# A hybrid decoder layer on one core: the MLP's up-projection as seven block products per pair of output tiles, in eighths

## The chip, the cores and the metric

One NeuronCore of one Trainium2 chip runs the whole kernel in one launch. The metric is the device time of an execution in microseconds. A profiled execution gives, besides, a trace of every instruction on the core's engines: PE (TensorE; PEld is its weight load), DVE (VectorE), ACT (ScalarE), POOL (GpSimd) and SP (SyncE, which here only issues DMAs).

## The reference

One layer of a decoder, float32 throughout: RMSNorm, a combined input projection, block-sparse attention and an mLSTM side by side, an output projection, a squared-ReLU MLP, and a final norm. The change concerns the last part. It works on 512 prompt tokens and 8 sample tokens, 520 in all; D_MODEL is 1024 and D_FF is 4096:

```python
    x = x + mix @ w_out
    hn = rmsnorm(x, ln2_w)
    x = x + jnp.square(jax.nn.relu(hn @ w_up)) @ w_down
```

## The kernel before

**Three passes.** Every float32 operand of a large matmul is split in two parts that TensorE reads in its fp32r format: `hi`, written by ACT as a copy into that format, and `lo`, the rest, written by DVE (or POOL) as a subtraction. A product is then three matmuls of 128x128 weights into one PSUM bank (`three`, L682 to L688): hi with hi, the activation's lo with the weight's hi, and the activation's hi with the weight's lo. Activations lie transposed, 128 features by 520 tokens, so a matmul streams tokens: 256 of them (half 0) or 264 (half 1).

**Output projection.** Eight output tiles of 128 features (groups G_OUT + j, j = 0 to 7), each in two token halves of 24 matmuls. A half is a slot; the program has 72 slots, and the last ones, 64 to 71, are tiles j = 4 to 7. Slots take three PSUM banks in turn, so a slot waits until the slot three before it has been added into `xT` by DVE (`evac_out`, L2070; counted by `s_acc_evac`). Behind an evacuated tile comes the task `x2` of that j: ACT writes `act_hi` (L1443) and a square `x_sq` (L1449), DVE writes `act_lo` (L2041) and adds the square into `sq_sum` (L2049).

**MLP.** Four quarters of 1024 hidden features. A quarter is 8 up tiles and 8 down tiles, each 8 k-steps times 2 halves times 3 passes, 48 matmuls (`main`, L716). The first up tile waits until all 72 slots are evacuated (`bank_free`), and is done k by k as `act_lo` comes. After it TensorE sums the squares over features (`sums_of_squares`, L1075), DVE scales the sums (L2111), POOL takes the power -1/2 (L1512), and TensorE spreads the result over partitions in the middle of the second tile (`norm_to_rows`, L1086); DVE copies it to `rstd2` (L2114). An up tile's PSUM is read by DVE with a ReLU and the factor `rstd2` into `relu` (L2132), squared twice by ACT (`relu2` L1484 and `h_hi` L1485), and `h_lo` is made by POOL (L1617). A down tile's PSUM is added into `xT` by DVE (L2076).

**Weights.** SP loads 1 MB at a time, 1024 rows by 256 columns, into one of two `raw` buffers. Each gives two weight tiles of 128x1024 elements, split by ACT (`weight_hi`, L1174) and DVE (`weight_lo`, L1181) three tiles ahead of TensorE into four slots. In the output projection POOL makes the lo parts, also those of the first three MLP tiles.

Every engine runs its own instructions in the order in which the program writes them, and waits on semaphores. Quarters 0 to 2 are a hardware loop on most engines, so counts that are waited for there are worked out in registers.

Of the kernel before, what the change touches and what calls it, by code (L numbers as in the profile page):

```python
# [264 lines left out]


# [1944 lines left out]
```

## Time and profile before

| | us |
|---|---|
| median of 3 runs | 758.96 |
| lowest, highest | 757.63, 759.50 |
| the profiled execution, its own time | 759.6 |
| its span, first to last instruction | 757.5 |
| granted TensorE clock, mean over the span | 0.987 |

| engine | busy us | share of the span |
|---|---|---|
| PE | 719.7 | 95% |
| DVE | 363.6 | 48% |
| ACT | 252.3 | 33% |
| POOL | 217.3 | 29% |

The profiled execution lies 0.6 us above the median of the runs, and 2.1 us of it lie outside its span. A matmul's duration (some 280 ns) is longer than the distance from its start to the next one's start, since matmuls follow each other in a pipeline; the distance is what counts for time. DVE and ACT instructions overlap their successors a little too.

### The profile page before, as it was taken

How to read it: one execution, taken by the hardware profiler on the slowest of the kernel's cores; microseconds unless marked ns; L12 is line 12 of the kernel's file. 1: busy time of each engine (PE TensorE's matmuls, PEld its weight loads, DVE VectorE, ACT ScalarE, POOL GpSimd, SP SyncE). 2: the span in 40 equal slices, each digit the busy share in tenths (PEclk: the TensorE clock that was granted, in tenths of full speed). 3: DMA queues.
4: the chain of work that ended last, by engine and by line, in shares of the span. 5: the costliest groups of instructions: out<-in, count | busy, mean ns of one | idle time of the engine just before them, and what ended most of it. 6: DMA issues, size and time to landing. Idle time of an engine off the chain costs nothing.

```text
span 757.5 us, 14708 instructions
## 1 busy us (share of the span) xinstructions
PE 719.7 (95%) x5729; PEld 670.3 (88%) x5729; DVE 363.6 (48%) x657; ACT 252.3 (33%) x424; POOL 217.3 (29%) x154
## 2 busy tenths in 40 slices
PE   5999789797999999899999999999999999999997
PEld 5988678676868676589999999999999999999996
DVE  4387878775353446435434333334333433333343
ACT  5342544535353213215324311342124322233312
POOL 6226987812232244163222100221002200022001
PEclk9999999998999999999999999999999999999999
DMA  7616898634456959623123332322331332313102
GB/s 241 209 56 211 270 279 250 191 125 117 146 155 202 282 193 163 221 86 106 62 60 110 112 112 62 106 92 77 111 109 58 111 94 72 112 57 111 57 1 112
DMA packets 94772, 100.37 MB, mean 133 GB/s; under 512 B 5374, under 2 KB 76626, under 8 KB 94714
## 3 DMA queue, kind: packets, MB, share of 16 engines
q1 hardware_dynamic: 80710, 92.91, 39.5%
q10 hardware_dynamic: 14004, 6.67, 3.7%
q8 instruction: 39, 0.64, 0.3%
q14 instruction: 19, 0.16, 0.1%
HBM read 92.92 MB, written 6.64 MB: 131 GB/s over the span
## 4 chain that ended last, share of the span: by engine, by line
PE 82%; DVE 7%; DMA 3%; ACT 2%; issue 2%; POOL 2%; SPq 1%; ACTq 0%; DVEq 0%; POOLq 0%
PE acc L684 23%; PE acc L685 22%; PE acc L686 22%; PE acc L1000 2%; DVE w_lo L1181 2%; DMA kv<-in_cache_v_dram 1%; PE scr L1050 1%; PE scr L931 1%; PE scr L944 1%; PE scr L1025 1%; ACT w_hi L1174 1%; DMA kv<-in_cache_k_dram 1%; PE scr L1038 1%; POOL sm_t L1512 1%; PE scr L775 1%
## 5 line engine op out<-in xcount | busy, mean ns | idle before, releaser
L684 PE MATMUL acc<-act_hi,w_hi 128*128 128x256 f32 (+1 forms) x928 | 269.1, 290 | 1.7 <-DVE zT L2056 1.1
L685 PE MATMUL acc<-act_lo,w_hi 128*128 128x256 f32 (+1 forms) x928 | 263.9, 284 | 0.0
L686 PE MATMUL acc<-act_hi,w_lo 128*128 128x256 f32 (+1 forms) x928 | 263.5, 284 | 0.0
L684 PEld LDWEIGHTS acc<-act_hi,w_hi 128*128 128x128 f32 x928 | 176.9, 191 | 9.1 <-issue 5.8
L685 PEld LDWEIGHTS acc<-act_lo,w_hi 128*128 128x128 f32 x928 | 176.9, 191 | 0.0
L686 PEld LDWEIGHTS acc<-act_hi,w_lo 128*128 128x128 f32 x928 | 176.4, 190 | 0.0
L1181 DVE TENSOR_TENSOR w_lo<-raw,w_hi 128x1024 fp32r<-128x1024 f32 x77 | 111.8, 1452 | 102.9 <-ACT w_hi L1174 102.5
L1174 ACT ACTIVATE w_hi<-raw 128x1024 fp32r<-128x1024 f32 x100 | 105.0, 1052 | 150.7 <-PE acc L686 147.2
L684 PE MATMUL acc<-h_hi,w_hi 128*128 128x264 f32 (+1 forms) x512 | 145.1, 283 | 0.0
L685 PE MATMUL acc<-h_lo,w_hi 128*128 128x264 f32 (+1 forms) x512 | 144.7, 283 | 0.0
L686 PE MATMUL acc<-h_hi,w_lo 128*128 128x264 f32 (+1 forms) x512 | 144.6, 282 | 0.0
L1617 POOL TENSOR_TENSOR h_lo<-relu,h_hi 128x520 fp32r<-128x520 f32 x32 | 42.1, 1316 | 277.3 <-ACT h_hi L1485 277.3
L684 PEld LDWEIGHTS acc<-h_hi,w_hi 128*128 128x128 f32 x512 | 96.6, 189 | 0.0
L685 PEld LDWEIGHTS acc<-h_lo,w_hi 128*128 128x128 f32 x512 | 96.5, 188 | 0.0
L686 PEld LDWEIGHTS acc<-h_hi,w_lo 128*128 128x128 f32 x512 | 96.3, 188 | 0.0
L1560 POOL TENSOR_TENSOR prod<-kv,Qb 128x1024 f32<-128x1024 f32 x32 | 82.9, 2617 | 42.6 <-DVE S L1759 25.2
L1181 POOL TENSOR_TENSOR w_lo<-raw,w_hi 128x1024 fp32r<-128x1024 f32 x23 | 54.9, 2390 | 105.6 <-ACT w_hi L1174 105.6
L2076 DVE TENSOR_TENSOR xT<-acc,xT 128x256 f32<-128x256 f32 x64 | 27.2, 428 | 84.7 <-PE acc L686 84.7
L1484 ACT ACTIVATE relu<-relu 128x520 f32<-128x520 f32 x32 | 20.4, 639 | 125.0 <-DVE relu L2132 125.0
L2056 DVE TENSOR_TENSOR zT<-acc,rstd 128x264 f32<-128x264 f32 (+1 forms) x56 | 23.5, 422 | 55.8 <-PE acc L686 52.7
L2132 DVE SCALAR_TENSOR_TENSOR relu<-acc,rstd 128x256 f32<-128x256 f32 x64 | 26.7, 421 | 40.1 <-PE acc L686 40.1
L684 PE MATMUL acc<-mix,w_hi 128*128 128x264 f32 (+1 forms) x128 | 37.7, 294 | 4.6 <-DVE mix L2022 3.2
(304 smaller groups left out, 823.1 us busy)
## 6 DMA issues: line engine op xcount, KB each, us to landing
kv<-in_cache_k_dram SPq DMA_DIRECT2D x64, 256.0 KB, 3.2
kv<-in_cache_v_dram SPq DMA_DIRECT2D x64, 256.0 KB, 3.5
raw<-in_w_up_dram SPq DMA_DIRECT2D x16, 1024.0 KB, 5.4
raw<-in_w_down_dram SPq DMA_DIRECT2D x16, 1024.0 KB, 5.1
raw<-in_w_in_dram SPq DMA_DIRECT2D x14, 512.0 KB, 6.0
raw<-in_w_in_dram SPq DMA_DIRECT2D x7, 1024.0 KB, 6.2
x_tok<-in_x_prompt_dram SPq DMA_DIRECT2D x8, 512.0 KB, 8.0
raw<-in_w_out_dram SPq DMA_DIRECT2D x4, 1024.0 KB, 7.5
```

The source lines that it names most:

```text
L684: pe.matmul(out, w_hi[:, slot, k, :], hi[k][:, cols], start=(n == 0), stop=False)
L685: pe.matmul(out, w_hi[:, slot, k, :], lo[k][:, cols], start=False, stop=False)
L686: mm = pe.matmul(out, w_lo[:, slot, k, :], hi[k][:, cols], start=False, stop=(n == KT - 1))
L1000: pe.matmul(acc[c:c + 32, 3, :], S_wide[:, b % 4, j, :], kv[:, j, :], start=(b % 4 == 0 and r == 0), stop=(b % 4 == 3 and r == 1)).then_in ...
L1174: act.activation(w_hi[:, slot, :, :], raw[:, r_slot, :, side * P:(side + 1) * P], ACT.Copy)\
L1181: eng.tensor_tensor(w_lo[:, slot, :, :], raw[:, r_slot, :, side * P:(side + 1) * P], w_hi[:, slot, :, :].bitcast(F32), ALU.subtract).then_ ...
L1484: act.activation(relu2[:, t % 2, :], relu[:, t % 2, :], ACT.Square)
L1560: pool.tensor_tensor(prod[:, n % 2, :].rearrange("p (j n) -> p j n", j=2), kv[:, 2 * c:2 * c + 2, :], Qb[:, b % 2:b % 2 + 1, :].to_broadca ...
L1617: pool.tensor_tensor(h_lo[:, t, :], relu2[:, t % 2, :], h_hi[:, t, :].bitcast(F32), ALU.subtract).then_inc(s_hs_lo, 1)
L2056: dve.tensor_tensor(zT[:, g, cols], acc[:, i % 3, 0:width(half)], rstd1[:, cols], ALU.mult)\
L2076: dve.tensor_tensor(x, acc[:, 2 * side + half, 0:width(half)], x, ALU.add).then_inc(s_acc_evac, 1)
L2132: dve.scalar_tensor_tensor(out=relu[:, t % 2, cols], in0=acc[:, 2 * (t % 2) + half, 0:width(half)], scalar=0.0, in1=rstd2[:, cols], op0=AL ...
```

## The change

Tokens are split in two halves of 260, the 1024 input features in two halves of four k-steps, and output tiles are taken in pairs. A pair is then a 2x2 by 2x2 block product. Before it took 8 block products of 12 matmuls (96 matmuls); now it takes 7 (84 matmuls), with sums of blocks on both sides (Strassen's scheme in the form with fewest sums):

- Weights: four sums of 128x512 blocks per pair (`w_sum`, DVE). A unit is now a 128x512 block or sum; ACT and DVE split each unit (`unit_hi`, `unit_lo`) into a ring of 11, and each unit serves one product of a pair or a half k-range of a down tile.
- Activations: in the task `x2` ACT also writes a scaled copy `xsc`, and for j = 4 to 7 DVE forms three sums of 128x260 (`t_tmp`), each of which ACT and DVE split too (`t2`, `t3`, `t4`); for j = 0 to 3 there is one difference (`t1_tmp`).
- Results: each product has a PSUM bank of its own (eight banks in turn). ACT copies the first to `p_copy`, and DVE makes seven additions of 128x260 per pair into `tmp0` and `tmp1`; the ReLU then reads these from SBUF, 520 wide.
- The MLP runs in eighths of 512 hidden features: up 0, up 1, down 0, up 2, down 1, and so on to down 5, up 7, and a last down phase over eighths 6 and 7 together. Down phases 0 to 5 accumulate over four k-steps only, so there are twice as many additions into `xT` for their features.
- The first 11 units are split in slots 65 to 71 of the output projection (`EARLY`), all of them by DVE. POOL has no weight split of the MLP any more.
- `sums_of_squares` now stands behind the third product, `norm_to_rows` behind the fifth.

```diff
-            def quarter(i, last):
...
+PAIR = ("A11", "A12", "S2", "S3", "S1", "S4", "A22")
+ORDER = [(what, side) for side in range(2) for what in PAIR]
+SUMS = {0: 1, 1: 2, 2: 3, 3: 4}
...
+PHASES = [("up", 0), ("up", 1)]
+for _d in range(6):
+    PHASES += [("down", _d)] + ([("up", _d + 2)] if _d < 6 else [])
+PHASES += [("last", 6)]
+RING = 11
...
+EARLY = {0: 65, 1: 65, 2: 66, 3: 66, 4: 67, 5: 68, 6: 68, 7: 70, 8: 70, 9: 71, 10: 71}
...
@@ PE
+            def up(e, i=0):
+
+                for m, (what, side) in enumerate(ORDER):
+                    n = FIRST["up", e] + m
+                    out = mlp_bank(BANKS["up", e, m][0])[:, 0:MH_TOK]
+                    bank_free("up", e, m, i)
+                    pe.wait_ge(s_u_lo, n + 1 + PER_LOOP * i)
+                    hi, lo = OPERAND[what]
+                    for k in range(4):
...
+                        pe.matmul(out, u_hi[n % RING][:, k, :], hi[k], start=(k == 0), stop=False)
+                        pe.matmul(out, u_hi[n % RING][:, k, :], lo[k], start=False, stop=False)
+                        mm = pe.matmul(out, u_lo[n % RING][:, k, :], hi[k], start=False,
+                                       stop=(k == 3))
+                    mm.then_inc(s_u_done, 1)
+                    if e == 0 and m == 2:
+                        sums_of_squares()
+                    if e == 0 and m == 4:
+                        norm_to_rows()
...
@@ DVE, task x2 from j = 4 on
+                        dve.tensor_tensor(t_tmp[:, 0, :], xsc[j][:, H1], xsc[k][:, H1], ALU.subtract).then_inc(s_t, 1)
+                        dve.wait_ge(s_t, made + 1)
+                        dve.tensor_tensor(t_tmp[:, 1, :], t_tmp[:, 0, :], xsc[k][:, H0], ALU.add).then_inc(s_t, 1)
+                        dve.wait_ge(s_x2_hi, j + 1)
+                        dve.tensor_tensor(act_lo[:, j, :], xsc[j][:, :], act_hi[:, j, :].bitcast(F32), ALU.subtract)\
+                           .then_inc(s_x2_lo, 1)
+                        dve.wait_ge(s_t, made + 2)
+                        dve.tensor_tensor(t_tmp[:, 2, :], xsc[j][:, H0], t_tmp[:, 1, :], ALU.subtract).then_inc(s_t, 1)
...
@@ DVE, a unit
+            def unit_lo(n, i=0):
+
+                kind, e, m, r = UNITS[n]
+                dve.wait_ge(s_u_hi, n + 1 + PER_LOOP * i)
+                dve.tensor_tensor(u_lo[n % RING], unit_source(n), u_hi[n % RING].bitcast(F32), ALU.subtract)\
+                   .then_inc(s_u_lo, 1)
+                if kind == "up" and m % 7 in SUMS:
+                    w_sum_of(e, SUMS[m % 7], m // 7, i)
...
@@ DVE, up
+                    if n == 2:
+                        dve.wait_ge(s_sums_up, 1)
+                        dve.tensor_scalar(rs[:, 0:NT], scr[:, 2, 0:NT], 1.0 / D, EPS, ALU.mult, ALU.add)\
+                           .then_inc(s_rs2_ms, 1)
...
```

The order that results, at three places on DVE. First the end of the output projection before, from the last-but-two additions into `xT` (slots 69 to 71, tiles 6 and 7) to the norm's scaling and copy:

```order
L2070 TENSOR_TENSOR xT<-acc,xT 128x264 [waits scr_free2,scr_free0,half_done]
L2070 TENSOR_TENSOR xT<-acc,xT 128x256 [waits scr_free2,scr_free1,half_done]
L2041 SCALAR_TENSOR_TENSOR act_lo<-xT,par,act_hi 128x520 [waits x2_hi]
L2049 TENSOR_TENSOR sq_sum<-sq_sum,x_sq 128x520 [waits sq_added,x1_sq]
L2070 TENSOR_TENSOR xT<-acc,xT 128x264 [waits scr_free2,scr_free1,half_done]
L2041 SCALAR_TENSOR_TENSOR act_lo<-xT,par,act_hi 128x520 [waits x2_hi]
L2049 TENSOR_TENSOR sq_sum<-sq_sum,x_sq 128x520 [waits sq_added,x1_sq]
L2111 TENSOR_SCALAR rs<-scr 128x4 [waits scr_full]
L2112 TENSOR_SCALAR rs<-scr 8x1
L2114 COPY rstd_62<-scr 128x512 [waits scr_full]
```

Between the additions of slots 70 (256 wide) and 71 (264 wide) stand one `act_lo` and one square.

The same place now, from the splits of the early units 7 and 8 through the addition of slot 71 (L2381) into the task x2 of tile 7 (buffer numbers are kept; `w_lo` and `u_lo` are places of the ring):

```order
L2413 TENSOR_TENSOR w_lo_52<-raw_49,w_hi_51 128x512 [waits u_hi]
L2398 TENSOR_TENSOR w_sum0_183<-raw_49 128x512 [waits u_lo]
L2413 TENSOR_TENSOR w_lo_52<-raw_49,w_hi_51 128x512 [waits u_hi]
L2401 TENSOR_TENSOR w_sum1_184<-w_sum0_183,raw_49 128x512 [waits w_sum,u_lo]
L2381 TENSOR_TENSOR xT_95<-acc,xT_95 128x264 [waits scr_free2,scr_free1,half_done]
L2341 TENSOR_TENSOR t_tmp_119<-xsc7_64,xsc3_60 128x260 [waits xsc]
L2343 TENSOR_TENSOR t_tmp_119<-t_tmp_119,xsc3_60 128x260 [waits t]
L2345 TENSOR_TENSOR act_lo_54<-xsc7_64,act_hi_53 128x520 [waits x2_hi]
L2348 TENSOR_TENSOR t_tmp_119<-xsc7_64,t_tmp_119 128x260 [waits t]
L2353 TENSOR_TENSOR t2_lo_139<-t_tmp_119,t2_hi_138 128x260 [waits t_hi]
L2353 TENSOR_TENSOR t3_lo_141<-t_tmp_119,t3_hi_140 128x260 [waits t_hi]
L2353 TENSOR_TENSOR t4_lo_66<-t_tmp_119,t4_hi_142 128x260 [waits t,t_hi]
```

Two splits and two weight sums stand ahead of slot 71's addition, and the task of tile 7 behind it is eight instructions instead of two.

Second, what follows on DVE up to the scaling of the sums of squares (L2510, L2512), where before `rs` stood right behind the last `sq_sum`:

```order
L2360 TENSOR_TENSOR sq_sum_82<-sq_sum_82,x_sq_81 128x520 [waits sq_added,x1_sq]
L2413 TENSOR_TENSOR w_lo_52<-w_sum1_184,w_hi_51 128x512 [waits u_hi]
L2403 TENSOR_TENSOR w_sum2_185<-raw_49 128x512 [waits u_lo]
L2413 TENSOR_TENSOR w_lo_52<-w_sum2_185,w_hi_51 128x512 [waits u_hi]
L2406 TENSOR_TENSOR w_sum3_186<-raw_49,w_sum1_184 128x512 [waits w_sum,u_lo]
L2413 TENSOR_TENSOR u_lo0_116<-w_sum0_183,u_hi0_113 128x512 [waits u_hi]
L2473 TENSOR_TENSOR tmp0_68<-acc,p_copy_69 128x260 [waits p_copy,u_done]
L2413 TENSOR_TENSOR u_lo1_117<-w_sum3_186,u_hi1_114 128x512 [waits u_hi]
L2473 TENSOR_TENSOR p_sum_70<-acc,p_copy_69 128x260 [waits u_done]
L2413 TENSOR_TENSOR u_lo2_118<-raw_49,u_hi2_115 128x512 [waits u_hi]
L2510 TENSOR_SCALAR rs_163<-scr 128x4 [waits sums_up]
```

Five unit splits, two weight sums and two additions of products moved in front of `rs`, whose first row is the last shown.

Third, the steady loop on DVE. Before:

```order
L1181 TENSOR_TENSOR w_lo<-raw,w_hi 128x1024 [waits w_hi_ok]
L2128 ISA
L2132 SCALAR_TENSOR_TENSOR relu<-acc,rstd_62 128x256 [waits half_done]
L2128 REGISTER_ALU
L2132 SCALAR_TENSOR_TENSOR relu<-acc,rstd_62 128x264 [waits half_done]
L1179 REGISTER_ALU
L1181 TENSOR_TENSOR w_lo<-raw,w_hi 128x1024 [waits w_hi_ok]
L2128 ISA
```

And now, in the middle of an up phase in the loop:

```order
L2412 REGISTER_ALU
L2413 TENSOR_TENSOR w_lo<-raw_d,w_hi 128x512 [waits u_hi]
L2482 REGISTER_ALU
L2473 TENSOR_TENSOR p_sum<-acc,p_copy 128x260 [waits u_done]
L2412 REGISTER_ALU
L2413 TENSOR_TENSOR w_lo<-raw_d,w_hi 128x512 [waits u_hi]
L2489 REGISTER_ALU [waits u_done]
L2473 TENSOR_TENSOR p_sum<-acc,p_sum 128x260 [waits c_ok]
L2492 REGISTER_ALU [waits u_done]
L2473 TENSOR_TENSOR tmp_67<-acc,p_sum 128x260 [waits c_ok]
L2473 TENSOR_TENSOR p_sum_71<-acc,p_sum 128x260
L2412 REGISTER_ALU
```

Each wait in the loop takes register instructions in both; now there are more and shorter instructions between them.

## Rows read from the trace of the kernel before

**Rows 1.** Windows: start:end, length; busy us (instructions) of PE, PEld, DVE, ACT, POOL; PEclk; DMA

```profile
353.50:373.50 20.00, 20.00 (x168) 19.87 (x166) 10.31 (x16) 9.55 (x14) 9.27 (x4) 1.00 0.33 107
374.00:750.00 376.00, 375.69 (x3133) 375.24 (x3133) 145.17 (x210) 105.09 (x138) 44.34 (x35) 1.00 0.26 82
```

**Rows 2.** Timeline of PE, both ends of a half tile: start us, duration us, instruction

```profile
500.38 0.28 PE L686 MATMUL acc<-act_hi,w_lo 128*128 128x256 f32 x1
500.50 0.28 PE L684 MATMUL acc<-act_hi,w_hi 128*128 128x264 f32 x1
...
503.29 0.28 PE L686 MATMUL acc<-act_hi,w_lo 128*128 128x264 f32 x1
503.41 0.28 PE L684 MATMUL acc<-act_hi,w_hi 128*128 128x256 f32 x1
```

**Rows 3.** DVE by line and shape, 400 to 725 us: xcount | busy us, mean ns | idle before

```profile
L1181 DVE TENSOR_TENSOR w_lo<-raw,w_hi 128x1024 fp32r<-128x1024 f32 x58 | 79.1, 1363 | 89.4 <-ACT w_hi L1174 89.4
L2132 DVE SCALAR_TENSOR_TENSOR relu<-acc,rstd 128x264 f32<-128x264 f32 x29 | 12.5, 432 | 38.6 <-PE acc L686 38.6
L2076 DVE TENSOR_TENSOR xT<-acc,xT 128x264 f32<-128x264 f32 x28 | 12.1, 433 | 57.8 <-PE acc L686 57.8
```

**Rows 4.** DVE by line and shape, whole span, inputs both in SBUF

```profile
L2017 DVE TENSOR_TENSOR zT<-zT 128x512 f32<-128x512 f32 x4 | 2.7, 684 | 0.0
...
L1899 DVE TENSOR_TENSOR S<-S,gate 128x256 f32<-128x256 f32 x2 | 0.9, 426 | 0.1
```

**Rows 5.** ACT and POOL by line and shape, 400 to 725 us

```profile
L1174 ACT ACTIVATE w_hi<-raw 128x1024 fp32r<-128x1024 f32 x57 | 59.9, 1051 | 107.5 <-PE acc L686 107.5
...
L1485 ACT ACTIVATE h_hi<-relu 128x520 fp32r<-128x520 f32 x29 | 18.0, 622 | 0.0
...
L1617 POOL TENSOR_TENSOR h_lo<-relu,h_hi 128x520 fp32r<-128x520 f32 x29 | 38.2, 1316 | 264.9 <-ACT h_hi L1485 264.9
```

**Rows 6.** Timeline of POOL and DVE: splits beside a POOL instruction and alone

```profile
499.63 1.32 POOL L1617 TENSOR_TENSOR h_lo<-relu,h_hi 128x520 fp32r<-128x520 f32 x1 [4.45 <-ACT h_hi L1485]
...
500.54 1.49 DVE L1181 TENSOR_TENSOR w_lo<-raw,w_hi 128x1024 fp32r<-128x1024 f32 x1 [2.26 <-ACT w_hi L1174]
...
429.85 1.23 DVE L1181 TENSOR_TENSOR w_lo<-raw,w_hi 128x1024 fp32r<-128x1024 f32 x1 [0.66 <-ACT w_hi L1174]
```

**Rows 7.** Timeline of DVE and PE, end of the output projection

```profile
357.15 0.68 DVE L2049 TENSOR_TENSOR sq_sum<-sq_sum,x_sq 128x520 f32<-128x520 f32 x1
357.76 0.42 DVE L2070 TENSOR_TENSOR xT<-acc,xT 128x264 f32<-128x264 f32 x1
...
370.70 0.42 DVE L2070 TENSOR_TENSOR xT<-acc,xT 128x256 f32<-128x256 f32 x1 [2.41 <-PE acc L686]
371.04 0.97 DVE L2041 SCALAR_TENSOR_TENSOR act_lo<-xT,par,act_hi 128x520 fp32r<-128x520 f32 x1
...
373.62 0.43 DVE L2070 TENSOR_TENSOR xT<-acc,xT 128x264 f32<-128x264 f32 x1 [1.00 <-PE acc L686]
...
374.15 0.36 PE L684 MATMUL acc<-act_hi,w_hi 128*128 128x256 f32 x1 [0.57 <-issue]
```

**Rows 8.** Norm of the MLP's input: chain (PE rows), then timeline of DVE and POOL

```profile
380.15 0.91 PE scr L1075 x10
...
384.10 1.20 PE scr L1086 x10
...
381.10 0.16 DVE L2111 TENSOR_SCALAR rs<-scr 128x4 f32<-128x4 f32 x1 [4.88 <-PE scr L1075]
...
385.02 0.69 DVE L2114 COPY rstd<-scr 128x512 f32<-128x512 f32 x1 [3.71 <-PE scr L1086]
...
381.46 1.52 POOL L1512 TENSOR_TENSOR rs<-rs,power 128x4 f32<-128x4 f32 x2 [9.99 <-DVE rs L2112]
```

**Rows 9.** Windows around an idle stretch of PE, columns as in the first group

```profile
168.00:175.00 7.00, 3.11 (x19) 1.77 (x17) 6.58 (x17) 0.00 (x0) 1.68 (x1) 1.00 0.00 0
175.00:183.00 8.00, 7.54 (x32) 6.87 (x33) 3.00 (x11) 4.14 (x11) 1.27 (x5) 0.57 0.61 164
```

More of the change, by code:

```diff
@@ new lines, with banks @@
+PREPARE = preparations()
+def banks():
+    use, last = {}, {b: ("out", N_HALVES) for b in range(3)}
+    last.update({b: ("scr", b - 4) for b in range(4, 8)})
+    for kind, e in PHASES:
+        if kind == "up":
+            for m, (what, side) in enumerate(ORDER):
+                b = m % 8
+                use[kind, e, m] = b, last.get(b)
+                last[b] = (("copy", 2 * e + side + 1) if what == "A11" else ("sum", 14 * e + 7 * side + READS[what]))
+                if e == 0 and m == 4:
+                    last[6] = last[7] = "rows", 2
+        else:
+            for j in range(16):
+                b = j % 4 if kind == "last" else (6 + j) % 8
+                use[kind, e, j] = b, last.get(b)
+                last[b] = "down", 16 * e + j + 1
+    return use
@@ L267 @@
+BANKS = banks()
+BANK_RATE = {"copy": 4, "sum": 28, "down": 32}
+for (_kind, _e, _n), (_b, _last) in BANKS.items():
+    if _kind != "last" and (_kind, _e) in PHASES[3:7]:
+        _b2, _last2 = BANKS[_kind, _e + 2, _n]
+        assert _b == _b2 and _last[0] == _last2[0] and _last2[1] - _last[1] == BANK_RATE[_last[0]]
+EARLY = {0: 65, 1: 65, 2: 66, 3: 66, 4: 67, 5: 68, 6: 68, 7: 70, 8: 70, 9: 71, 10: 71}
+N_DOWN = 16 * 6 + 16
 TASKS, JOBS = plan()
@@ new lines, in down_part @@
+            def down_part(b, half, n, k, first, last, signal):
+                out, cols = mlp_bank(b)[:, 0:MH_TOK], (H0, H1)[half]
+                w = u_hi[n % RING][:, k % 4, :], u_lo[n % RING][:, k % 4, :]
+                pe.matmul(out, w[0], h_hi[:, k, cols], start=first, stop=False)
+                pe.matmul(out, w[0], h_lo[:, k, cols], start=False, stop=False)
+                mm = pe.matmul(out, w[1], h_hi[:, k, cols], start=False, stop=last)
+                if signal is not None:
+                    mm.then_inc(signal, 1)
@@ L1458, in y_scale, with phase @@
+            def phase(kind, e, i=0):
+                if kind == "up":
+                    up(e, i)
+                else:
+                    down(kind, e, i)
             def y_scale(i):
@@ L2146, in add_squares, with phase @@
+            def phase(kind, e, i=0):
+                if kind == "up":
+                    up(e, i)
+                elif kind == "down":
+                    down(e, i)
+                else:
+                    down_last()
             def add_squares(j):
```

574 lines of the change are left out of this document (425 added, 149 removed).

## The prediction

> **What bounds the kernel now.** I read three views in this order. First the windows: from 374 to 750 us, the whole MLP, TensorE is busy 375.7 of 376 us at a granted clock of 1.00, and DVE 145, ACT 105, POOL 44 [rows 1]. So in this stretch a matmul that goes is time that goes, as long as no other engine takes over. Second the timeline of PE: matmuls of 264 tokens start 0.121 us apart (24 of them from 500.50 to 503.41), those of 256 some 0.12, and between two halves, where the PSUM bank changes, there is no gap: 503.29 to 503.41 [rows 2]. Third the end of the output projection. There too PE is busy without a gap [rows 1], DVE adds slot 71 into xT at 373.62, as soon as it is there, and the first MLP matmul starts at 374.15 after 0.57 us of idling [rows 7]. DVE is at half load in that stretch, so the last addition finds it free.
>
> **What goes.** 16 pairs lose one block product of 12 matmuls: 192 matmuls. At 260 tokens each takes 0.120 us, so 23.0 us. Nothing else lies on PE in the MLP: 2880 matmuls of 0.120 are 345.6 us against 368.6.
>
> **What DVE has to do for it, steady state.** I cost DVE by the distance of starts. 128x520 takes 0.61 us (357.15 to 357.76), 128x256 takes 0.34 (370.70 to 371.04) [rows 7]; recorded durations are 0.07 to 0.08 longer, and the same whether an input is PSUM or both are SBUF: 0.43 for 256 to 264 [rows 3, 4], and 0.68 for 512 [rows 4]. For one eighth (14 products, 8 down units):
> - 22 unit splits of 512 at 0.61: 13.4
> - 8 weight sums at 0.61: 4.9
> - 14 additions of products at 0.34: 4.8
> - 4 ReLUs of 520 at 0.61: 2.4
> - 16 additions into xT at 0.34: 5.4
>
> That is 30.9 us on 64 instructions. PE needs (168 + 192) x 0.120 = 43.2 us for the same. POOL's four h_lo (1.32 us each [rows 5]) slow DVE when it reads two SBUF inputs: the split that overlapped one by 0.41 us (500.54 to 500.95) took 1.49 where a lone one takes 1.23 [rows 6], so about two thirds of an overlap is lost. At worst that is two thirds of 5.3 us, 3.5, and DVE stands at 34.4 of 43.2, or 80%. The ring of 11 units is full when an up phase starts, and as 8 units are split there while 14 are used, five are left at its end; so DVE may fall behind by five units, and eight PSUM banks by about as many products, so peaks inside an eighth don't reach PE. ACT has 22 splits of about 0.55 (half of 1.05 [rows 5]), 8 squares of 0.62 and two copies: 18 us, no bound. So the 23.0 us are gained in full behind the start.
>
> The Trainium skill ("SBUF — State Buffer", section "SBUF: two separate sides") calls the port pair of VectorE and GpSimd an exclusive lock: the one that comes second blocks fully. By that rule all of the 0.41 us would have been lost where the trace has 0.26, and all 5.3 us of POOL would stand on DVE: 36.2 of 43.2. The sum is the same by both; the reserve below would be smaller.
>
> **The start of the MLP.** Here the new work meets a PE that has no other to do. The first product, like the first tile now, waits until all 72 slots are evacuated. Ahead of slot 71's addition DVE now has, from slot 65's addition on: 6 additions (2.0), 9 unit splits (5.5), 6 weight sums (3.7), the task x2 of tiles 4, 5, 6. One such task is five instructions of 260 that follow one another at 0.34, one more at 0.46 since the next waits for its result (0.43 plus the 0.03 of a semaphore), and two of 520: 3.4 us, so 10.2. And 1.4 us of waits for ACT: xsc of tile 6 can only start when slot 69 has been added (0.7), and the split of a weight sum waits for ACT's copy of it (0.7). Together 22.8 us. Slot 65's addition starts at 357.76 now [rows 7] and about 2.0 us later then, since in the tasks of tiles 2 and 3 ACT has two more instructions each (0.6 and 0.3), and POOL's last split there, pushed back by ACT, falls on DVE's two-input instructions. So slot 71 is added at 357.8 + 2.0 + 22.8 = 382.6 instead of 373.62 [rows 7], and PE starts at 383.1 instead of 374.15: **9.0 us lost**. Two of them fall earlier, where slot 70 waits for the bank of slot 67. POOL's splits of MLP tiles are gone, which the walk has already: DVE runs there undisturbed (act_lo took 0.97 beside POOL at 371.04 [rows 7]).
>
> **The norm.** PE does A11, A12, S2 (3 x 1.44), the sums (0.91 [rows 8]), S3 and S1, and is at norm_to_rows at 383.1 + 8.1 = 391.2. DVE: from 382.6 the addition, 1.0 us until xsc of tile 7 is there (0.73 on ACT), the task of tile 7 (3.4) to 387.2, then five splits, two weight sums, one wait of 0.7 and two product additions, 5.7, and `rs` at about 393.0. From `rs` to the end of POOL's power it is 381.10 to 382.98, 1.9 us [rows 8], so PE goes on at 394.9 to 395.0. **3.8 us lost.** Before, this chain lay behind a half tile: `rs` was ready at 382.98 and PE came at 384.10. Then PE spreads the rows (1.2), does S4, and product A22 needs a bank that DVE frees only when it has read S4's product and copied the rows: 0.2 + 0.34 + 0.61 + 0.2, **1.35 us lost**.
>
> **The end.** Down 6 and 7 follow up 7 at once. From the end of up 7 to the last h_lo: addition 0.6, ReLU 0.7, two squares on ACT 1.2, POOL 1.3, about 3.9 us. The last phase needs that tile only in its eighth k-step, after 42 matmuls or 5.0 us. No loss, 1.1 us in hand. The tail behind it is unchanged.
>
> **Sum.** -23.0 + 9.0 + 3.8 + 1.35 = -8.9 us. From the profiled execution's own 759.6 that gives 750.7; it lies 0.6 above the median of the runs, so the median becomes **750 us**, 1.2% less.
>
> **The clock.** PE idled from about 172 to 175 us, and in the next 8 us the granted clock was 0.57 [rows 9]: most of them at 1.2 GHz instead of 2.4. Before the first product PE will idle some 7 us at a stretch, so I expect such a stretch again. It slows products whose end nobody waits for: PE reaches norm_to_rows up to 3.4 us later, and that wait shrinks by as much. Only what exceeds 3.8 us would be lost. I take 0, with 0 to 3 us as its bounds.
>
> **Rivals.**
> 1. *DVE keeps up at the start.* If the waits for ACT vanish and the tasks of tiles 2 and 3 cost nothing, slot 71 is added 3.4 us earlier; if the norm's wait also shrinks, as it starts earlier relative to the sums, the time is 743 to 745. For it: every duration I added is one of the trace. Against it: to lose nothing DVE would have to do 22.8 us in 15.9. A gain of the full 23 us (736) is only possible if PE need not wait, and the order rules that out.
> 2. *The start costs more.* Sixty instructions with a wait each, ACT and DVE alternately: 0.05 us more each is 3 us; the clock's 3 us come on top: 753 to 757.
> 3. *DVE becomes the bound in the loop.* The loop has register instructions ahead of most waits, and there are 64 short instructions per eighth where there were half as many. In the old loop a register instruction between a split and a ReLU costs nothing that shows. The reserve is (43.2 - 34.4) / 64 = 0.14 us per instruction (0.11 by the skill's rule). From 0.16 on the whole gain is gone; at 0.18 DVE needs 45.9 us per eighth, 2.7 x 6.5 eighths = 17.6 us are lost, and the kernel is **slower: 768**.
> 4. *Short groups cost PE.* The MLP has 208 groups of 12 matmuls and 16 of 24 instead of 128 of 24, each with one or two waits in registers. If the start of a short group cost 0.05 us, 208 x 0.05 = 10 us would be lost: 760, no change. Against it: no gap where the bank changes now [rows 2]. A matmul whose tokens start at column 260 instead of 256 is not in the trace; if it took the time of 264 columns, that is 2880 x 0.001, 3 us.
>
> **Chances.** Forecast (745.5 to 754): 0.60. Rival 1 (740 to 745.5): 0.12. Rival 2 (754 to 758): 0.12. Rival 3: 0.09. Rival 4: 0.07. A measurement of this kernel can tell about 0.3%, 2.3 us, from no change: faster than 756.7 are the forecast, rival 1 and most of rival 2, together 0.82; within 0.3% 0.07; slower 0.11. The range 740 to 758 leaves out rivals 3 and most of 4.
>
> **What would show it.** In the new trace: products 1.44 us apart and no wait of PE from the second pair on; DVE at 70 to 80% in the loop; the first product at about 383 with 7 us of idling before it, ended by DVE's addition L2381; norm_to_rows (L1225) waiting for POOL; 1.3 us ahead of the seventh product; slot 70 waiting 2 us. I would be wrong if PE waits for `u_lo` or a bank in the loop (rival 3), if group starts show gaps (rival 4), or if slot 71 is added before 379.

## The result and the profile after

| | before | after |
|---|---|---|
| median, us | 758.30 (4 runs, 757.46 to 759.50) | 749.43 (4 runs, 748.75 to 750.73) |
| the profiled execution, its span | 759.6, 757.5 | 749.51, 747.8 |
| ratio after / before, 95% interval | | 0.9884 (0.9863 to 0.9905) |

The change gains 8.9 us, 1.2%: faster, clear of the noise, and by about what was forecast. The windows of after (columns as in [rows 1]):

```profile
374.00:750.00 376.00, 359.03 (x2972) 357.52 (x2970) 284.33 (x529) 150.53 (x276) 53.44 (x37) 0.98 0.28 90
376.00:384.00 8.00, 1.60 (x7) 1.60 (x8) 7.09 (x16) 4.70 (x10) 0.00 (x0) 0.63 0.41 130
384.00:392.00 8.00, 8.00 (x53) 7.96 (x52) 7.24 (x16) 4.78 (x10) 0.00 (x0) 0.73 0.00 1
436.00:650.00 214.00, 214.00 (x1790) 214.00 (x1789) 170.76 (x320) 87.57 (x161) 31.81 (x21) 1.00 0.31 98
```

Against [rows 1] DVE went from 145 to 284 us and PE from busy throughout to 359 of 376. The last row is the loop: PE busy 214.00 of 214, DVE 80%. All that PE loses lies near the start of the MLP. PE's waits from 350 to 760 us, in all four (engine, line it waited in, releaser: us in total, times, longest):

```profile
PE acc L1304 <- DVE xT L2381: 7.0, 1, 7.0
PE acc L853 <- DVE xT L2381: 2.7, 1, 2.7
PE scr L1304 <- DVE rstd L2460: 1.3, 1, 1.3
PE scr L1225 <- POOL rs L1798: 1.0, 1, 1.0
```

In order of time they are slot 70, the first product, `norm_to_rows` and product A22. Timeline of PE and DVE there (start us, duration us, instruction, [idle before <- what ended it]), which answers to [rows 7, 8]:

```profile
369.35 0.39 PE L853 MATMUL acc<-mix,w_hi 128*128 128x256 f32 x1 [2.74 <-DVE xT L2381]
...
381.92 0.43 DVE L2381 TENSOR_TENSOR xT<-acc,xT 128x264 f32<-128x264 f32 x1
...
382.40 0.59 PE L1304 MATMUL acc<-act_hi,u_hi 128*128 128x260 f32 x1 [7.02 <-DVE xT L2381]
...
383.44 0.42 PE L1305 MATMUL acc<-act_lo,u_hi 128*128 128x260 f32 x1
383.65 0.42 PE L1306 MATMUL acc<-act_hi,u_lo 128*128 128x260 f32 x1
...
389.47 1.07 PE L1215 MATMUL scr<-ones,sq_sum 128*128 128x1 f32 x10
...
392.35 0.16 DVE L2510 TENSOR_SCALAR rs<-scr 128x4 f32<-128x4 f32 x1
...
394.65 1.47 PE L1225 MATMUL scr<-ident,rs 128*128 128x128 f32 x10 [0.99 <-POOL rs L1798]
...
399.06 0.39 PE L1304 MATMUL scr<-t_hi,w_hi 128*128 128x260 f32 x1 [1.32 <-DVE rstd L2460]
...
740.98 1.53 PE L1255 MATMUL scr<-ident,xT 128*128 128x128 f32 x12
```

Matmuls start 0.21 us apart at 383.5 (granted clock 0.63 and 0.73 in the two windows above, so 1.2 GHz for part of the time). The last row is PE's final block, in before this row:

```profile
750.64 1.53 PE L1116 MATMUL scr<-ident,xT 128*128 128x128 f32 x12
```

So it comes 9.66 us earlier. Not all of that is the change's: POOL's split near 344 us, which the change leaves alone, starts at 344.30 in before and at 343.09 in after. In the other profiles below slot 70's matmuls start anywhere from 367.5 to 371.6 us. From here on times of one profile are therefore counted from that start (369.35 in after): this is what I call **behind slot 70**, and PE's final block stands 371.63 behind it.

### The profile page after: what moved, and what is told of

Its sections match the earlier page's. It is cut to its first block, busy times and chain, and to the rows that moved or that the text cites. A ratio compares the mean times of both kernels' runs of the same rounds, so it can differ in the third digit from the quotient of the medians.

```text
span 747.8 us, 15197 instructions
## 1 busy us (share of the span) xinstructions
PE 701.4 (94%) x5537; PEld 651.6 (87%) x5537; DVE 510.5 (68%) x996; ACT 301.4 (40%) x576; POOL 217.7 (29%) x151
## 4 chain that ended last, share of the span: by engine, by line
PE 76%; DVE 7%; issue 7%; DMA 3%; ACT 3%; POOL 2%; SPq 1%; ACTq 0%; DVEq 0%; POOLq 0%
PE acc L853 6%; PE acc L854 5%; PE acc L1319 5%; PE acc L855 5%; PE acc L1318 5%; PE acc L1320 5%; PE acc L1305 4%; PE acc L1304 4%; PE acc L1306 4%; PE scr L1319 3%; PE scr L1318 3%; PE scr L1304 3%; PE scr L1320 3%; PE scr L1306 3%; PE scr L1305 3%
## 5 line engine op out<-in xcount | busy, mean ns | idle before, releaser
L853 PE MATMUL acc<-act_hi,w_hi 128*128 128x256 f32 (+1 forms) x416 | 124.9, 300 | 0.6 <-DVE zT L2367 0.5
L854 PE MATMUL acc<-act_lo,w_hi 128*128 128x256 f32 (+1 forms) x416 | 120.1, 289 | 0.0
L855 PE MATMUL acc<-act_hi,w_lo 128*128 128x256 f32 (+1 forms) x416 | 119.9, 288 | 0.0
L853 PEld LDWEIGHTS acc<-act_hi,w_hi 128*128 128x128 f32 x416 | 81.3, 196 | 7.4 <-issue 4.8
L854 PEld LDWEIGHTS acc<-act_lo,w_hi 128*128 128x128 f32 x416 | 81.5, 196 | 0.0
L855 PEld LDWEIGHTS acc<-act_hi,w_lo 128*128 128x128 f32 x416 | 81.1, 195 | 0.0
L1318 PE MATMUL acc<-h_hi,w_hi 128*128 128x260 f32 x200 | 56.8, 284 | 0.0
L1319 PE MATMUL acc<-h_lo,w_hi 128*128 128x260 f32 x200 | 56.6, 283 | 0.0
L1320 PE MATMUL acc<-h_hi,w_lo 128*128 128x260 f32 x200 | 56.5, 282 | 0.0
L1395 ACT ACTIVATE w_hi<-raw 128x1024 fp32r<-128x1024 f32 x36 | 37.8, 1054 | 35.8 <-PE acc L855 31.9
```

The lines of the kernel that those rows point to most:

```text
L853: pe.matmul(out, w_hi[:, slot, k, :], hi[k][:, cols], start=(n == 0), stop=False)
L854: pe.matmul(out, w_hi[:, slot, k, :], lo[k][:, cols], start=False, stop=False)
L855: mm = pe.matmul(out, w_lo[:, slot, k, :], hi[k][:, cols], start=False, stop=(n == KT - 1))
L1318: pe.matmul(out, w[0], h_hi[:, k, cols], start=first, stop=False)
L1319: pe.matmul(out, w[0], h_lo[:, k, cols], start=False, stop=False)
L1320: mm = pe.matmul(out, w[1], h_hi[:, k, cols], start=False, stop=last)
```

## Experiments

Each changes one thing of the kernel after, unless it says otherwise. Its runs are compared with runs of before on the same chip; e0, e2, e3 and e4 ran on one chip, e5 to e8 on a second, e1, e9 and e11 on a third. Two sets of the unchanged kernel after differ by 2.3 us (749.43, and 751.69 in e0), with intervals that overlap; so for effects of a microsecond the distances inside a profile say more than the medians.

| kernel | median us | ratio to before (95%) | first product / rs / norm_to_rows / A22 / final block, us behind slot 70 |
|---|---|---|---|
| after | 749.43 | 0.9884 (0.9863 to 0.9905) | 13.05 / 23.00 / 25.30 / 29.71 / 371.63 |
| e0_after | 751.69 | 0.9910 (0.9886 to 0.9934) | 13.05 / 23.00 / 25.21 / 29.62 / 371.51 |
| e1_rows_first | 748.77 | 0.9864 (0.9845 to 0.9882) | 13.06 / 23.01 / 25.22 / - / 369.98 |
| e2_defer78 | 753.59 | 0.9931 (0.9911 to 0.9951) | 10.64 / 23.84 / 26.05 / 32.87 / 376.15 |
| e3_rs_first | 749.27 | 0.9870 (0.9845 to 0.9895) | 13.05 / 21.08 / 24.00 / 28.30 / 370.90 |
| e4_all_three | 745.42 | 0.9819 (0.9799 to 0.9840) | 10.64 / 18.41 / 21.28 / 24.47 / 367.26 |
| e11_best2 | 744.47 | 0.9816 (0.9791 to 0.9842) | 10.05 / 17.97 / 20.21 / - / 366.13 |
| e9_best_warm | 744.94 | 0.9808 (0.9789 to 0.9827) | 10.06 / 17.97 / 20.25 / - / 366.20 |
| e5_keep_warm | 751.16 | 0.9905 (0.9886 to 0.9923) | 15.06 / 23.03 / 25.24 / 30.92 / 372.81 |
| e10_pool_lo | 753.76 | 0.9927 (0.9901 to 0.9954) | 14.94 / 24.88 / 27.09 / 31.50 / 373.42 |
| e6_load1 | 750.84 | 0.9891 (0.9859 to 0.9924) | 13.05 / 23.00 / 25.22 / 29.64 / 371.55 |
| e7_load2 | 780.06 | 1.0279 (1.0256 to 1.0302) | 13.05 / 23.00 / 25.21 / 30.64 / 403.10 |
| e8_short_a22 | 734.64 | 0.9686 (0.9668 to 0.9703) | 13.06 / 23.02 / 25.38 / 29.79 / 355.14 |

(A dash: no wait marks the place.) **e0_after** is the kernel after, once more beside the others:

> The changed kernel again, as the measure for the others of this job. Both theories: about 749.4 us. In its trace: the first product some 7 us late behind DVE's addition of slot 71, the rows of the norm waiting 1 us for POOL, the seventh product 1.3 us for rstd2; the loop without a wait of PE.

Its waits are 5.5, 2.78, 1.07 and 1.32 us: the steps repeat to a tenth, apart from the first one, which is shorter since PE did slots 70 and 71 at a lower clock (0.72 from 370 to 374 us); the first product starts at the same distance.

### Are the start's losses those of DVE's queue?

**e2_defer78.** Two early units (with their weight sums) leave DVE's queue ahead of slot 71's addition.

```diff
-EARLY = {..., 7: 70, 8: 70, 9: 71, 10: 71}
+EARLY = {..., 7: 71, 8: 71, 9: 71, 10: 71}
```

> Units 7 and 8 (two splits, two weight sums, 2.4 us of DVE) are made behind slot 71's addition and tile 7's sums instead of ahead of them. Theory A (DVE's work up to the norm's rs and rows is one serial chain, and the order inside it changes nothing): the first product starts 2.4 us earlier, rs does not, PE's wait at norm_to_rows grows by 2 to 3 us, total within 1 us of the changed kernel (749 to 750.5). Rival B (what is lost is PE's late start): 2.4 us faster, 747.

The first product comes 2.41 us earlier, 4 DVE instructions of 0.60: that much of the account is right. But in the profile the final block comes 4.5 us later, beyond both theories. The median is 4.2 us above that of after and 1.9 above that of e0, which ran beside it; there the intervals overlap, so the medians show no more than that nothing was gained. The same four instructions now stand ahead of `rs`, so PE waits for them at `norm_to_rows`:

```profile
397.55 2.60 PE L1225 MATMUL scr<-ident,rs 128*128 128x128 f32 x10 [4.65 <-POOL rs L1798]
```

and behind this second idle stretch the clock fell again (windows of e2, columns as in [rows 1]):

```profile
392.00:400.00 8.00, 3.35 (x18) 2.92 (x16) 6.96 (x16) 2.61 (x5) 1.87 (x2) 0.83 0.41 128
400.00:408.00 8.00, 6.68 (x31) 6.36 (x32) 2.49 (x6) 1.79 (x3) 1.31 (x1) 0.53 0.02 6
```

`norm_to_rows` took 2.60 us instead of 1.47, and A22 came 3.2 us later than in after. Behind A22 another 1.4 us go. A stall that was only moved cost more, in this execution, than where it was. It is the slowest of e2's six (756.2 against 752.6 to 755.0), and whether the others have the second fall of the clock isn't known.

**e3_rs_first.** `rs` moves ahead of the splits of units 9 to 13 (9 and 10 are no longer early).

```diff
-EARLY = {..., 7: 70, 8: 70, 9: 71, 10: 71}
+EARLY = {..., 7: 70, 8: 70}
...
+                    if n == 2:
+                        dve.wait_ge(s_sums_up, 1)
+                        dve.tensor_scalar(rs[:, 0:NT], scr[:, 2, 0:NT], ...
                     for u in PREPARE["up", e, m]:
                         unit_lo(u, i)
-                    if n == 2:
-                        dve.wait_ge(s_sums_up, 1)
-                        dve.tensor_scalar(rs[:, 0:NT], scr[:, 2, 0:NT], ...
```

> Units 9 and 10 with their two weight sums go behind rs, rs goes ahead of unit 11, and the steps of the first eighth make up for it later (1 unit a step, 2 in three steps). The first product starts as before. Theory A: rs comes some 3 us earlier, PE no longer waits at norm_to_rows (-1.0 in the trace), and DVE is not late for S4's product, so 1 to 3 us faster: 746.5 to 748.5. Rival B (late start alone): no change, 749.4. Rival C (DVE is so full that the ring runs dry in the first two eighths): PE waits for u_lo around the twentieth product, no gain or a loss.

`rs` is 1.9 us earlier and is now released by PE's sums; PE doesn't wait at `norm_to_rows`, which comes 1.3 us earlier, and A22 comes 1.4 us earlier. So that stall was DVE's queue ahead of `rs`. The final block is only 0.73 us earlier: 0.7 us are given back in the second eighth, around 428 us, where PE waits 0.22 for `w_lo` and starts a few matmuls further apart than 0.12. That is rival C in small: the splits put off leave the ring empty there. The median (749.27) lies outside theory A's range, on rival B's number, and 2.4 us below e0's; it can't tell the two.

**e1_rows_first.** DVE copies the norm's rows before it adds S4's product, not after.

```diff
+                    if n == 5:
+                        norm_rows()
                     if what != "A11":
                         dve.wait_ge(s_u_done, n + 1 + PER_LOOP * i)
```

> Edit: DVE copies the norm's rows (rstd2) ahead of the addition of S4's product and not behind it, in the first up phase alone. In the trace of after, product A22 starts 1.32 us late, ended by the copy of the rows (L2459). Theory A (each stall of the start is paid by itself): with the copies first, A22 waits for the bank only, 0 to 0.4 us, and 0.5 to 1.3 us are gained: 748.1 to 748.9. Rival B (what comes behind pays it back, the ring of units is not full): a new wait of PE for w_lo behind A22 and no gain.

The wait of 1.32 us ahead of A22 is gone and the final block stands 1.65 us earlier; the median (748.77) lies in theory A's range. The order of two DVE instructions was worth the whole 1.3 us.

**e4_all_three.** The edits of e1, e2 and e3 together.

> The changes of e2 and e3 together, and the copies of rstd2 ahead of the addition of S4's product. Theory A: the start 2.4 us earlier, no wait at norm_to_rows, the wait of the seventh product 0.5 instead of 1.3: 3.5 to 4.5 us faster than the changed kernel, 745 to 746. Rival B: 2.4 us faster, 747. Rival C: waits for u_lo in the second eighth, no gain.

4.4 us earlier in the profile, and 4.0 us in the median (6.3 against e0, which ran beside it). A22 comes 5.2 us earlier: the 2.4 us of e2, the stall at `norm_to_rows` (1.0), that ahead of A22 but for 0.2 (1.1), and some 0.7 more, 0.4 of it since PE's first three products took 6.66 us instead of 7.07. Then 0.9 us are given back in the second eighth, around a wait of 0.40 for `w_lo`, as in e3. Units 7 and 8 and their sums still stand ahead of `rs` in e4; what left the queue ahead of it are the splits of units 9 to 13 and two sums. So DVE comes to `rs` before PE's sums are there:

```profile
387.93 0.68 DVE L2401 TENSOR_TENSOR w_sum<-w_sum,raw 128x512 f32<-128x512 f32 x1
...
389.68 0.16 DVE L2508 TENSOR_SCALAR rs<-scr 128x4 f32<-128x4 f32 x1 [0.39 <-PE scr L1215]
```

PE's waits in e4:

```profile
PE acc L1304 <- DVE xT L2381: 4.6, 1, 4.6
PE acc L853 <- DVE xT L2381: 2.8, 1, 2.8
PE scr L1304 <- DVE w_lo L2413: 0.4, 1, 0.4
PE scr L1304 <- DVE rstd L2460: 0.2, 1, 0.2
```

**e11_best2.** e4, and unit 6 too goes from slot 68 to slot 71.

> Edit: e4_all_three, and unit 6 too is split behind slot 71 of the output projection instead of slot 68. Its split (0.61 us of DVE) no longer stands ahead of slot 71's addition. Theory A (the first product waits for DVE's queue alone): first product 0.6 us earlier, at about 10.0 us behind slot 70's start instead of 10.6; but behind it rs waits for PE's sums, which come earlier by as much, so 0 to 0.6 us are gained on 745.4. Rival B (ring now binds): the same split comes behind, DVE is late with rs or with the units for A22, and the time is 745 to 746.

The first product is 0.59 us earlier and the final block 1.1 us; the ratio (0.9816 against 0.9819) can't tell the two. The wait for `w_lo` in the second eighth is 0.7 us now (0.2 in e3, 0.4 in e4): each split that is put off is paid for in part there.

**e10_pool_lo** undoes one part of the change: the lo parts of units 0 to 8 are POOL's.

```diff
@@ POOL, slot s
+                for u in EARLY:
+                    if u < 9 and EARLY[u] == s:
...
+                        pool.wait_ge(s_u_hi, u + 1)
+                        pool.tensor_tensor(u_lo[u % RING], unit_source(u), u_hi[u % RING].bitcast(F32),
+                                           ALU.subtract).then_inc(s_u_lo, 1)
@@ DVE, slot s, units 0 to 8: the weight sum alone
-                        unit_lo(n)
+                                w_sum_of(0, SUMS[m], 0, 0)
```

> Edit: the changed kernel, with the lo parts of the early units 0 to 8 (slots 65 to 70) made by POOL instead of DVE, as the split before the change had it; DVE keeps the weight sums. DVE's queue between the additions of slots 65 and 71 loses 9 splits of 0.61 us, 5.5 us of its 22.8. POOL gets 9 of about 1.25 us, 11 us, nearly all of it beside DVE instructions with two SBUF inputs. Theory A (my prediction's: two thirds of an overlap are lost on DVE): 5.5 us won, 7.4 lost, so slot 71 is added about 2 us later than in after, and 1 to 3 us are lost overall: 751 to 753. Rival B (the Trainium skill, SBUF - State Buffer, section SBUF: two separate sides: the port pair is an exclusive lock, the second comer blocks fully): 11 us lost on DVE, slot 71 5.5 us later, 754 to 756. Rival C (two inputs beside POOL cost nothing once both engines are short of nothing else): slot 71 is added 5 us earlier and the time is 744 to 747. The durations of DVE's and POOL's instructions there say which.

From slot 65's to slot 71's addition DVE takes 25.4 us (357.34 to 382.71), 2.5 us more than in after (359.07 to 381.92), though 5.5 us of work left it. In total that is theory A's size, and the median stands between A and B. The single instructions however say B (e10, POOL first, then DVE):

```profile
373.50 1.29 POOL L1901 TENSOR_TENSOR w_lo<-w_sum,w_hi 128x512 fp32r<-128x512 f32 x1 [3.27 <-ACT w_hi L1710]
374.75 1.29 POOL L1901 TENSOR_TENSOR w_lo<-raw,w_hi 128x512 fp32r<-128x512 f32 x1
```

```profile
373.55 0.76 DVE L2389 TENSOR_TENSOR xT<-acc,xT 128x264 f32<-128x264 f32 x2
374.78 1.55 DVE L2349 TENSOR_TENSOR t_tmp<-xsc,xsc 128x260 f32<-128x260 f32 x1 [0.47 <-ACT xsc L1670]
376.36 0.43 DVE L2351 TENSOR_TENSOR t_tmp<-t_tmp,xsc 128x260 f32<-128x260 f32 x1
```

The two additions at 373.55, which read one PSUM input, ran beside POOL at their usual 0.42. The subtraction at 374.78, two SBUF inputs, overlapped POOL's by 1.26 us (to 376.04) and took 1.55 instead of 0.43: 1.12 lost, all of the overlap but 0.14. It has seven such rows, which lose 0.86 to 1.12 each, 7.0 us in all. The Trainium skill ("SBUF — State Buffer", section "SBUF: two separate sides") has an exclusive lock in which the second comer blocks fully; the trace agrees, but for 0.14 us. My total came out near only because part of POOL's some 11.5 us (nine of 1.26 to 1.29) fell beside additions from PSUM or where DVE waited for ACT (0.47 ahead of the subtraction above).

### Does the fallen clock cost anything?

**e5_keep_warm.** 54 unused matmuls on PE ahead of the first product.

```diff
+            for n in range(54):
+                pe.matmul(scr[:, 3, 0:256], mix[:, HI[n % 4], 0:P], mix[:, HI[n % 4], 0:256], start=True, stop=True)
```

> PE does 54 additional matmuls of 256 columns into a PSUM bank that nobody reads, between slot 71 and the first product, where it idles otherwise; everything else as in the changed kernel. They take about 6.5 us and keep PE busy. Theory A (the slow clock behind the idle stretch costs nothing, since PE waits for the norm anyway): granted clock 1.00 through the first products, PE reaches norm_to_rows some 3 us earlier and waits there 4 us instead of 1, total as the changed kernel, 749 to 751; if that 4 us wait brings the clock down again, up to 752. Rival B (the slow clock costs its 3 us): 746.5.

PE ran the first products at a clock of 1.00, and `rs` stood at 23.03 behind slot 70 and `norm_to_rows` at 25.24, as in after (23.00, 25.30). But the wait there grew to 1.68 only, not to the 4 us expected, as the additional matmuls themselves held the first product back:

```profile
376.66 6.63 PE L1373 MATMUL scr<-mix 128*128 128x256 f32 x54
383.13 0.28 PE L1304 MATMUL acc<-act_hi,u_hi 128*128 128x260 f32 x1
```

That is 15.06 behind slot 70, where DVE's addition would have let it go at 13.05: PE had done slots 70 and 71 at a low clock (0.61 from 368 to 376 us) and came late to them. So PE was at its sums only 0.75 us earlier than in after, and of the 2.75 us of the slow stretch this run tests 0.75; these were worth nothing. A22 came 1.2 us later: the clock was low behind the norm this time (0.83 and 0.74 from 392 to 400). The median lies between both sets of the kernel after.

**e9_best_warm.** e11, and 30 such matmuls.

> Edit: e11_best2 and 30 more matmuls on PE, results unused, just ahead of the first product. In e5_keep_warm such matmuls gained nothing, and theory A says why: there rs waited for DVE, so PE's half clock in its first products was covered. In e4 and e11 rs waits for PE's sums (L1215) instead. If theory A holds, the full clock pays now: products A11, A12, S2 take 4.3 us instead of about 6.5, so 1.5 to 2.5 us gained on e11_best2: 743 to 744. Rival B (DVE is as late as PE even there): rs within 0.7 us of where it stands in e11, and no gain.

Here the additional matmuls end in time: the first product is at 10.06 behind slot 70 (10.05 in e11), and PE reaches its sums 1.49 us earlier (14.47 against 15.96). It waits 1.57 us at `norm_to_rows` for it, and that stands where it did. Theory A fell, and rival B held: `rs` in e11 stands on DVE's queue again, not on PE's sums; rows of e11, then of e9:

```profile
385.14 0.42 DVE L2473 TENSOR_TENSOR p_sum<-acc,p_copy 128x260 f32<-128x260 f32 x1
385.48 0.15 DVE L2508 TENSOR_SCALAR rs<-scr 128x4 f32<-128x4 f32 x1
```

```profile
388.18 0.43 DVE L2476 TENSOR_TENSOR p_sum<-acc,p_copy 128x260 f32<-128x260 f32 x1
388.52 0.16 DVE L2511 TENSOR_SCALAR rs<-scr 128x4 f32<-128x4 f32 x1
```

`rs` follows the addition at DVE's own distance of 0.34, 17.97 us behind slot 70 in both, and `norm_to_rows` is at 20.21 and 20.25. I had read "released by PE" in e4 (a wait of 0.39 us), and overlooked that unit 6's split, put behind slot 71 in e11, took up that wait. What bounds the start of e11 is DVE, with PE next to it: PE came to `norm_to_rows` at 20.21, just when POOL was through.

In e3 and e4 it is otherwise, and there the low clock wasn't free. From `rs` to `norm_to_rows` it is 2.2 to 2.3 us wherever PE waits for POOL, but 2.92 in e3 and 2.87 in e4: PE came 0.6 to 0.7 us late. `rs` had waited 0.48 and 0.39 us for PE's sums besides. So about 1 us of their start is PE's, whose first three products took 6.92 and 6.66 us instead of 4.32; in e11 they took 5.91, which is part of its gain over e4. No run takes the slow stretch out of e3 or e4 alone.

### Is the loop as far from DVE's bound as worked out?

**e6_load1, e7_load2.** One more DVE reduction behind each unit split of the loop, over 260 elements in e6 and 520 in e7.

```diff
+                if n >= FIRST["up", 2]:
+                    dve.tensor_reduce(t_tmp[:, 2, n:n + 1], t_tmp[:, 0, :], AX.X, ALU.add)
```

> One additional DVE reduction of 260 elements behind each unit split from unit 36 on (22 per eighth, 140 in all, 0.34 us each, 7.5 us per eighth); its result is used by nothing. DVE's load goes from 34.4 to 41.9 us per eighth of 43.2. Theory A (reserve of 8.8 us per eighth): no change, at most 1 us: 749 to 751. Rival C (the loop is nearly DVE-bound already, registers and waits included): 5 to 15 us slower.

> As the run before, with reductions of 520 elements (0.61 us, 13.4 us per eighth). DVE's load is 47.8 us per eighth against 43.2 of PE. Theory A: DVE becomes the bound, 4.6 us lost in each of some five and a half eighths, 22 to 28 us slower: 771 to 778. If the reserve were larger than I reckon: less. Rival C: 45 us or more slower.

Windows of e6 and of e7, 436 to 650 us:

```profile
436.00:650.00 214.00, 214.00 (x1790) 214.00 (x1789) 202.36 (x426) 86.14 (x160) 29.84 (x20) 1.00 0.31 99
```

```profile
436.00:650.00 214.00, 200.55 (x1619) 199.54 (x1618) 204.13 (x380) 75.40 (x139) 24.91 (x17) 0.96 0.28 89
```

e6 puts DVE at 95% and PE still never waits; the final block stands at 371.55 behind slot 70, as in after. e7 asks for more than PE's time: DVE stays at 95%, PE at 94%, waiting for DVE in five stretches of up to 4.1 us from 436 to 650 us:

```profile
PE acc L1304 <- DVE xT L2386: 13.4, 5, 4.1
```

and the kernel is slower than before. Rival 3's mechanism exists. The busy share doesn't show how near it is, since e6, where DVE costs nothing, and e7, where it is the bound, both stand at 95%; what is left to DVE in both are mainly its waits for ACT (7.8 and 6.4 us of the 214). The limit lies between the loads, 41.9 and 47.8 us per eighth of 43.2.

The 780 us are above theory A's 771 to 778. Behind A22 e7 takes 30.5 us more than after. PE's waits are 19.3 of them: the 13.4 above, 3.4 more for DVE and 2.5 for `h_lo` behind 650 us. Much of the rest is the clock, which fell behind four of the stalls; one of those windows:

```profile
504.00:512.00 8.00, 8.00 (x54) 8.00 (x54) 7.27 (x15) 2.06 (x4) 0.00 (x0) 0.76 0.42 133
```

These are 54 matmuls instead of 69. It and its like behind the three other stalls (54 to 57 matmuls) hold 6.2 us. Theory A had counted DVE's time alone.

**e8_short_a22.** Product A22 does one k-step of four: in 16 pairs 9 matmuls fewer, 144 in all.

```diff
+                        if what == "A22" and k > 0:
+                            continue
```

> The seventh product of each pair (A22) is done over one k-step instead of four: 9 matmuls fewer in each of 16 pairs, 144 in all (its sums are then wrong, nothing else changes). Theory A (PE is the bound in every up phase): 144 x 0.120 = 17.3 us less, of which the first pair's 1.1 us may go into a wait: 731.5 to 734. Rival C (DVE sets the pace of the up phases): clearly less than 17 us, below 10.

The final block stands 16.5 us earlier behind slot 70 and the median 14.8 us lower, against 144 x 0.120 = 17.3. PE's waits are those of after. The median is 0.6 us above theory A's range. So a matmul less in the loop is worth its distance with DVE as loaded as it is, to within a microsecond or two; rival 4 (short groups cost PE), which now had groups of 3, shows at most the 0.8 us that is missing, and 0.4 of these lie in one place of the 16: at 426.24, where PE goes from a short group over to the first down phase, 0.49 and 0.19 us pass between starts instead of 0.12.

## Why the prediction was right, point by point

- **What goes (-23.0): right.** In the loop matmuls of 260 tokens start 0.12 us apart, also over group ends. From the first product to the final block there were 376.49 us in before (374.15 to 750.64) and there are 358.58 (382.40 to 740.98), 17.9 less: that is 23.0 less the 1.0 and 1.3 of the two waits and the 2.75 us by which the low clock stretched the first three products (36 matmuls from 382.40 to 389.47, 7.07 us instead of 4.32).
- **DVE in the loop: right.** Worked out 34.4 of 43.2 us, 80%; measured 170.76 of 214, 80%, on 320 instructions, 64.6 per 43.2 us. That both say 34.4 or 34.5 us is partly luck: the 3.5 us allowed for POOL were a worst case, and the splits beside POOL lost some 1.9 per eighth (an estimate: 25 at 968 and 33 at 795 ns in the mean, where undisturbed ones take 684, over 250 us), while recorded durations run some 0.08 us on into each idle stretch, which the count of starts leaves out. Rival 3's 0.14 us of overhead per instruction isn't there. The reserve is real: e6 used 6.4 us per eighth of it (31.6 us more in 214) without loss, and e7, which asked for 13.4, found its end.
- **POOL's effect: wrong in its form.** "About two thirds of an overlap is lost" was read off one pair [rows 6]: 0.26 of 0.41. What is lost is the overlap less some 0.14, and this holds for 0.41 (0.27) as well. It also works the other way round, which I had left out. In after:

```profile
467.35 0.68 DVE L2413 TENSOR_TENSOR w_lo<-raw_d,w_hi 128x512 fp32r<-128x512 f32 x1
...
468.71 1.05 DVE L2413 TENSOR_TENSOR w_lo<-raw_d,w_hi 128x512 fp32r<-128x512 f32 x1
```

```profile
465.30 1.78 POOL L1902 TENSOR_TENSOR h_lo<-relu,h_hi 128x520 fp32r<-128x520 f32 x1 [28.93 <-ACT h_hi L1719]
467.59 1.62 POOL L1902 TENSOR_TENSOR h_lo<-relu,h_hi 128x520 fp32r<-128x520 f32 x1 [0.51 <-ACT h_hi L1719]
```

  POOL at 465.30 and 467.59 came second, beside DVE splits; the one at 467.59 came while DVE held the port (to 468.03, 0.44) and took 0.30 more than its 1.32; DVE at 468.71 came while POOL held it (to 469.21, 0.50) and took 0.37 more than 0.68. It didn't change the sum, since the reserve was there.
- **The start (+9.0): right.** From slot 65's to slot 71's addition 22.8 us were worked out and 22.85 measured. Slot 65's addition was to come 2.0 us later, at 359.8; it is at 359.07, or 360.3 with the 1.2 us by which this execution is ahead. The first product is at 382.40, or 383.6 so corrected, against 383.1: 9.5 us lost instead of 9.0.
- **The norm (+3.8) and the clock (0): right together, within 0.1 us.** `rs` was forecast at 393.0 and is at 392.35 (393.6 corrected). PE came to `norm_to_rows` 2.75 us late by the clock and waits 0.99 there, together 3.7: as the prediction said, the wait absorbs the slow stretch. In after `rs` follows DVE's split without idling, 1.8 us after PE's sums have ended (389.47 and 1.07 more), so it didn't wait for PE. e5 takes 0.75 us of the delay away and e9, on top of e11, 1.5, and in both `rs` and `norm_to_rows` stay where they are. That holds where DVE is the later one; in e3 and e4 it is not.
- **A22 (+1.35): right**, 1.32, and e1 gets it back.
- **The end (0): right**, PE doesn't wait there.
- **The sum** by what was measured: -23.0 + 9.5 + 3.7 + 1.3 = -8.5 us; behind the point where they stand 1.2 apart the profiles differ by 8.45. The medians differ by 8.9. That the median came within 0.6 us of the forecast is partly luck, as the same kernel gave 751.69 in e0.

Nothing of rivals 1, 2 and 4 came: the waits for ACT at the start are there (0.76 and 0.46 ahead of slot 71's addition, 0.80 behind it), and sixty instructions with waits cost no 0.05 us more each.

What stays open: how the 0.5 us at slot 65 divides between ACT and POOL, and whether the 0.4 us at one of 16 short groups in e8, and the 0.4 that are found nowhere, are a cost of groups or that execution's own, and where the rest of e7's loss lies.

## What to carry to other kernels

A cut in the bound engine's work is worth its full count where the engine that pays for it keeps a reserve (here DVE's load went from 34 to 42 of 43.2 us per eighth for nothing, with 5 to 11 units and several banks of slack by the prediction's count), and is given back where the new work has to be done first, in a queue in which the next stage's release stands at the end. There, walk the queue instruction by instruction with start-to-start distances; and when moving work past one release, look at the next one that it then stands ahead of. e2 moved four instructions so, and its profile lost 4.5 us. e4 moved the same four to the same place, but put `rs` ahead of seven other instructions and the norm's rows ahead of an addition, and gained 4.4. What is put off so has to be done soon after: in e4 0.9 us of it came back in the second eighth. e4 and e11 beat both kernels: 745.4 and 744.5 us, 1.8% below before.

## What the runs showed of the hardware

- VectorE with two SBUF inputs and GpSimd exclude each other: whoever comes second waits for the other's end, but for 0.14 us (the rows above). From 450 to 700 us of after two groups of DVE's splits, some of which fall beside POOL's `h_lo`, take 968 and 795 ns in the mean where a group that doesn't takes 686, and POOL's `h_lo` went from 1316 ns [rows 5] to 1588:

```profile
L2413 DVE TENSOR_TENSOR w_lo<-raw,w_hi 128x512 fp32r<-128x512 f32 x33 | 25.7, 795 | 0.0
L2413 DVE TENSOR_TENSOR w_lo<-raw_d,w_hi 128x512 fp32r<-128x512 f32 x25 | 24.2, 968 | 0.0
L2413 DVE TENSOR_TENSOR w_lo<-w_sum,w_hi 128x512 fp32r<-128x512 f32 x32 | 21.5, 686 | 3.7 <-ACT w_hi L1710 3.6
```

```profile
L1902 POOL TENSOR_TENSOR h_lo<-relu,h_hi 128x520 fp32r<-128x520 f32 x24 | 37.9, 1588 | 219.5 <-ACT h_hi L1719 219.3
```

- TensorE's clock can fall twice within 20 us: in e2 it is 0.76 and 0.81 in the two windows of 8 us from 376 on, with the first idle stretch (4.60 us), and 0.53 behind the second (4.65 us). After the wait of 0.99 us in the kernel after it stayed at 1.00 from 392 to 400. The length of the last stall alone doesn't tell: behind PE's stall at slot 70 (2.74 to 2.79 us) the clock from 368 to 376 us was 1.00 in after, e2, e4 and e9 and 0.79 in e0, e1 and e3. In e7 it was 0.76 to 0.81 behind stalls of 3.80, 4.08, 2.67 and 3.39 us, and 1.00 behind one of 2.35.
